# A convolutional gated MLP: the input scaled by 1/rms once, taps read from PSUM, and four of five down granules as seven block products

## What is computed

```
h = _rmsnorm(x, ffn_norm_g[l])
u = jnp.einsum('bsd,df->bsf', h, w_up[l])          # 1024 -> 2 * 2816
u = _causal_dwconv(u, conv_w[l], conv_b[l])        # y[t] = b + w0 u[t-2] + w1 u[t-1] + w2 u[t]
gate, val = jnp.split(u, 2, axis=-1)
x = x + jnp.einsum('bsf,fd->bsd', jax.nn.silu(gate) * val, w_down[l])
```

## Time and profile before

| | |
|---|---|
| median of 3 runs | 1955.98 us (1955.34 to 1956.61) |
| span of the profiled execution, first to last instruction | 1955.1 us |
| TensorE busy, share of the span | 1937.1 us, 99% |
| VectorE busy | 1419.4 us, 73% |
| ScalarE busy | 854.3 us, 44% |
| this MLP, with what lies just around it | 440 to 830 us of the span |

### The profile page before, as it was taken

The page is one execution under the profiler, slowest core; times in us unless marked ns, Lnnn a source line. Parts: engine busy times, 40 slices in busy tenths (PEclk is TensorE's granted clock), DMA queues, the critical chain, the costliest instruction groups (busy, mean ns, idle before and its releaser), DMA issues.

```text
span 1955.1 us, 24513 instructions
## 1 busy us (share of the span) xinstructions
PE 1937.1 (99%) x9769; PEld 1623.6 (83%) x9769; DVE 1419.4 (73%) x1983; ACT 854.3 (44%) x1343; POOL 123.8 (6%) x152
## 2 busy tenths in 40 slices
PE   9999999999999999999999999999999999999998
PEld 8887777888888888888888899998877888888886
DVE  6665687568656665846477788888898778887787
ACT  5453464335333334533222444444357655444443
POOL 1001240000000000000000010000024310000000
PEclk9999999999999999999999999999999999999999
DMA  5322212212323232332322432332223132332311
GB/s 177 108 87 65 89 63 87 86 43 88 108 91 104 87 107 87 108 108 87 108 72 80 137 106 87 112 116 76 76 62 105 44 118 68 127 108 87 108 65 65
DMA packets 139826, 181.14 MB, mean 93 GB/s; under 512 B 9792, under 2 KB 98496, under 8 KB 139712
## 3 DMA queue, kind: packets, MB, share of 16 engines
q1 hardware_dynamic: 137824, 178.04, 28.3%
q10 hardware_dynamic: 1632, 1.51, 0.2%
q0 software_dynamic: 256, 0.02, 0.0%
HBM read 177.44 MB, written 2.10 MB: 92 GB/s over the span
## 4 chain that ended last, share of the span: by engine, by line
PE 94%; DVE 3%; ACT 1%; issue 1%; POOL 0%; ACTq 0%; DVEq 0%; POOLq 0%
PE bank L751 21%; PE bank L753 21%; PE bank L752 20%; PE bank L1293 5%; PE bank L1291 5%; PE bank L1292 5%; PE bank L915 4%; PE bank L794 2%; PE bank L796 2%; PE bank L795 2%; PE bank L907 2%; PE bank L1005 1%; PE bank L993 1%; PE bank L1220 1%; DVE w_lo L1441 1%
## 5 line engine op out<-in xcount | busy, mean ns | idle before, releaser
L751 PE MATMUL bank<-h_hi,w_hi 128*128 128x512 f32 x1384 | 546.0, 395 | 2.1 <-DVE w_lo L1441 1.2
L753 PE MATMUL bank<-h_hi,w_lo 128*128 128x512 f32 x1384 | 539.2, 390 | 0.0
L752 PE MATMUL bank<-h_lo,w_hi 128*128 128x512 f32 x1384 | 538.8, 389 | 0.0
L2340 ACT ACTIVATE w_hi<-raw 128x1024 fp32r<-128x1024 f32 (+2 forms) x207 | 203.2, 1020 | 260.6 <-PE bank L753 207.3
L751 PEld LDWEIGHTS bank<-h_hi,w_hi 128*128 128x128 f32 x1384 | 259.9, 188 | 58.6 <-issue 3.0
L752 PEld LDWEIGHTS bank<-h_lo,w_hi 128*128 128x128 f32 x1384 | 260.0, 188 | 54.5 <-issue 2.1
L753 PEld LDWEIGHTS bank<-h_hi,w_lo 128*128 128x128 f32 x1384 | 259.8, 188 | 54.5
L1441 DVE TENSOR_TENSOR w_lo<-raw,w_hi 128x1024 fp32r<-128x1024 f32 (+2 forms) x195 | 235.9, 1241 | 34.0 <-ACT w_hi L2340 33.3
L751 PE MATMUL bank<-g_hi,w_hi 128*128 128x512 f32 (+1 forms) x460 | 177.9, 387 | 1.7 <-issue 1.0
L753 PE MATMUL bank<-g_hi,w_lo 128*128 128x512 f32 (+1 forms) x460 | 172.6, 375 | 0.0
L752 PE MATMUL bank<-g_lo,w_hi 128*128 128x512 f32 (+1 forms) x460 | 172.3, 375 | 0.0
(11 more groups left out here) (304 smaller groups left out, 3216.8 us busy)
## 6 DMA issues: line engine op xcount, KB each, us to landing
raw<-w SPq DMA_DIRECT2D x32, 1024.0 KB, 5.4
arena<-w SPq DMA_DIRECT2D x32, 1024.0 KB, 5.1
raw<-w_up SPq DMA_DIRECT2D x22, 1024.0 KB, 5.2
raw<-a_w_in SPq DMA_DIRECT2D x16, 1024.0 KB, 5.3
raw<-w_in SPq DMA_DIRECT2D x11, 1024.0 KB, 5.3
raw<-w_down SPq DMA_DIRECT2D x11, 1024.0 KB, 5.0
raw<-w_mkv SPq DMA_DIRECT2D x8, 1024.0 KB, 5.2
raw<-a_w_out SPq DMA_DIRECT2D x8, 1024.0 KB, 5.1
```

The source lines that it names most:

```text
L751: nc.tensor.matmul(dst, a_hi, b_hi, start=(k == 0), stop=False)
L752: nc.tensor.matmul(dst, a_hi, b_lo, start=False, stop=False)
L753: last = nc.tensor.matmul(dst, a_lo, b_hi, start=False, stop=(k == n - 1))
L2340: A(hi, src, ACT.Copy).then_inc(w_hi_done, 1)
```

## The change

- 1/rms is multiplied into `x * gain` once (8 tiles `h_scaled`), and `h_hi`, `h_lo` are made anew from it. The first pair still runs on the unscaled input, and its tiles are taken out with the multiplication. All later pairs run on the scaled input.
- The taps of these pairs are read from PSUM: ScalarE's last tap and VectorE's two others. VectorE's second one frees the bank (`tile_taken`).
- The down granules 0 to 3 are made of seven block products of 24 matmuls of 256 columns each, in the order P1, P2, P6, P4, P7, P5, P3. P3 and P4 are added to the residual at once, P5, P6 and P7 into sums in SBUF, P1 and P2 stay in banks; `gate_fold` adds them all at the end. Granule 4 and the 11th pair's chunk are made as before.

The diff, cut to its core. VectorE at the start, its taps, its place between the up tiles and the products of a granule (in `gate_granule`), the takes of the products, the fold, and what stands behind the granules:

```diff
+            def take_first_up():
+                def first_up(j):
                     take(lambda b: V.tensor_tensor(conv_u[:, j, 2:], b[:], rstd[:, 0, :], ALU.mult))
...
+                first_up(0)
+                scale_normed(range(0, 4))
+                first_up(1)
+                for j in range(2):
+                    gate_low("up", 0, j)
+                scale_normed(range(4, KT))
+                first_up(2)
+                for n in range(KT):
+                    low_half(h_lo[:, n, :], h_hi[:, n, :], h_scaled[:, n, :], None, h_ready)
+                first_up(3)
+                for j in range(2):
+                    gate_low("up", 1, j)
...
+            def up_tap(pair, j, between=lambda: None):
+                early = pair <= 2 * GATE_GRANULES
+                dve.wait_ge(act_out, acts.n + ((1, 2, 5, 6) if early else (1, 2, 3, 4))[j])
+                bank_of_up = tile_bank[tile.n % 4]
+                V.scalar_tensor_tensor(conv_y[:, j, 1:S], bank_of_up[:, 0:S - 1], w_col("conv_w1", pair, j),
+                                       conv_y[:, j, 1:S], ALU.mult, ALU.add).then_inc(tap_made, 1)
+                taps.n += 1
+                between()
+                dve.wait_ge(tap_made, taps.n)
+                take(lambda b: V.scalar_tensor_tensor(conv_y[:, j, 2:S], b[:, 0:S - 2], w_col("conv_w0", pair, j),
+                                                      conv_y[:, j, 2:S], ALU.mult, ALU.add))
...
+            def up_taps(pair):
+                for j in range(4):
+                    up_tap(pair, j, split_low if j % 2 else lambda: None)
...
+                up_tap(2 * n + 2, 2)
+                gate_low("P6", n)
+                up_tap(2 * n + 2, 3, lambda: gate_low("P4", n))
+                gate_low_left("P6", s2, lefts + 4)
...
+            def gate_take(n, name, t):
+                if name in ("P3", "P4"):
+                    dst = (by_half[1][0] if name == "P4" else by_half[0][1])[:, 2 * t:2 * t + 2, :]
+                    op = ALU.subtract if name == "P4" else ALU.add
+                    take(lambda bank: V.tensor_tensor(dst, dst, bank.rearrange("p (a b) -> p a b", b=256), op))
+                elif n == 0:
+                    take(lambda bank: V.tensor_copy(gate_sums[name][:, t, :], bank[:]))
+                else:
+                    take(lambda bank: V.tensor_tensor(gate_sums[name][:, t, :], bank[:], gate_sums[name][:, t, :], ALU.add))
...
+            def gate_fold():
+                p5, p6, p7 = [gate_sums[name].rearrange("p a (c n) -> p (a c) n", n=256) for name in ("P5", "P6", "P7")]
+                c11, c12, c21, c22 = by_half[0][0], by_half[0][1], by_half[1][0], by_half[1][1]
+                def in_order(dst, a, b):
+                    keep_order(V.tensor_tensor(dst, a, b, ALU.add))
+                dve.wait_ge(tile_taken, tile.n)
+                dve.wait_ge(gate_kept, 2 * GATE_GRANULES)
+                for dst in (c11, p6):
+                    for t in range(2):
+                        part = dst[:, 2 * t:2 * t + 2, :]
+                        in_order(part, KEPT["P1"][t].rearrange("p (a b) -> p a b", b=256), part)
+                settle()
+                for t in range(2):
+                    part = c11[:, 2 * t:2 * t + 2, :]
+                    V.tensor_tensor(part, KEPT["P2"][t].rearrange("p (a b) -> p a b", b=256), part, ALU.add)\
+                     .then_inc(gate_folded, 1)
+                in_order(c12, c12, p6)
+                in_order(p7, p7, p6)
+                settle()
+                in_order(c12, c12, p5)
+                in_order(c21, c21, p7)
+                in_order(c22, c22, p7)
+                settle()
+                keep_order(V.tensor_tensor(c22, c22, p5, ALU.add))
+                settle()
+                dve.wait_ge(gate_folded, 2)
...
+            gated_low(2 * GATE_GRANULES)
+            up_tap(9, 0)
+            gate_fold()
+            up_tap(9, 1, split_low)
+            up_tap(9, 2)
+            up_tap(9, 3, split_low)
+            gated(9)
+            gated_low(9)
+            up_taps(10)
+            gated(10)
             down(middle=lambda: gated_low(10))
             back("final, mix0")
```

ScalarE, high of a left operand, the place between the up tiles and the products of a granule, and pairs 9 and 10:

```diff
+            def gate_left_of(n, name, src, made_before, used):
+                if made_before:
+                    act.wait_ge(gate_left_made, 4 * n + made_before)
+                if used:
+                    act.wait_ge(*GATE_W.used_by[GATE_W.piece_at[used]])
+                A(left_form(g_hi, name), src, ACT.Copy).then_inc(gate_left_hi, 1)
...
+                up_tap(2 * n + 2, 2)
+                up_tap(2 * n + 2, 3)
+                gate_high("P6", n)
+                gate_high("P4", n)
+                gate_left_of(n, "P6", s2, 2, ("P1", n, 0))
...
+            def last_up(pair):
+                first = tile.n
                 for j in range(4):
                     if j % 2:
                         split_high()
...
+                    up_tap(pair, j)
```

TensorE:

```diff
+            def gate_product(n, name):
+                pe.wait_ge(w_split, GATE_W.lows(name, n))
+                pe.wait_ge(gate_left, 6 * n + GATE_LEFTS[name])
+                w_form = [GATE_W.ring(t, name, n).rearrange("p (k n) -> p k n", k=2) for t in (w_hi, w_lo)]
+                left = [left_form(t, name) for t in (g_hi, g_lo)]
+                kept = name in KEPT
+                if n == 0 and name == "P1":
+                    pe.wait_ge(std_done, stats.n)
+                for t in range(2):
+                    dst = (KEPT[name][t] if kept else next_bank())[:]
+                    for f in range(2):
+                        region = dst[:, 256 * f:256 * f + 256]
+                        cut = slice(P * (2 * t + f), P * (2 * t + f) + P)
+                        for k in range(2):
+                            (s_hi, s_lo), (m_hi, m_lo) = [x[:, k, cut] for x in w_form], [x[:, k, :] for x in left]
+                            begin = k == 0 and (n == 0 and f == 0 if kept else True)
+                            ends = k == 1 and (n == GATE_GRANULES - 1 or not kept)
+                            nc.tensor.matmul(region, s_hi, m_hi, start=begin, stop=False, skip_group_check=kept)
+                            nc.tensor.matmul(region, s_hi, m_lo, start=False, stop=False, skip_group_check=kept)
+                            last = nc.tensor.matmul(region, s_lo, m_hi, start=False, stop=ends, skip_group_check=kept)
+                    if not kept:
+                        full(last)
+                if kept:
+                    last.then_inc(gate_kept, 1)
...
+            for n in range(GATE_GRANULES):
+                for c in range(4 * n, 4 * n + 4):
+                    gate_up(c)
+                for name in PRODUCTS:
+                    gate_product(n, name)
+            for n in range(GATE_GRANULES, 5):
                 for c in range(4):
                     by_feature()
                 down()
```

More of the change, by code:

```diff
@@ L118, in weight_stream @@
     out += [g(0), v(0)]
-    for n in range(5):
+    before_gate = sum(item[0] not in ("tiles", "gate", "mlp1") for item in out)
+    out += [("gate", GATE_TILES)]
+    for n in range(GATE_GRANULES, 5):
         out += [g(2 * n + 1), v(2 * n + 1), g(2 * n + 2), v(2 * n + 2)] + down("w_down", n)
@@ L129, in weight_stream @@
         out += [first, ("tiles", 4 if n < 3 else 0), second]
-    not_shared = sum(item[0] not in ("tiles", "mlp1") for item in out)
+    not_shared = sum(item[0] not in ("tiles", "gate", "mlp1") for item in out)
     out += [("mlp1", MLP_TILES)]
@@ L135, in weight_stream @@
     out += [rows("b_w_o_2", c) for c in range(4)]
-    return out, not_shared
+    return out, not_shared, before_gate
 def build(nc, w, out):
@@ L772, in by_feature @@
                     parts = (range(0, 5), range(5, KT)) if j == 1 and between else (range(KT),)
+                    if passing and j == 1:
+                        parts = [range(k, k + 1) for k in range(KT)]
                     for part in parts:
@@ L775, in by_feature @@
                                          arrive if j == 0 else None, part)
-                        if part[-1] < KT - 1:
+                        if passing and j == 1:
+                            if part[-1] == KT - 1:
+                                tile.n += 1
+                                last.then_inc(tile_full, 1)
+                            else:
+                                last.then_inc(h_passed, 1)
+                        elif part[-1] < KT - 1:
                             between()
-                    full(last)
+                    if not (passing and j == 1):
+                        full(last)
                 if tiles == 2 or not pair:
@@ L2577, in _, with high_of_scaled, last_tap @@
             root(rstd[:, 0, :], None, stat_bank[:], None, D)
-            def up(granule):
+            def high_of_scaled():
+                for n in range(KT):
+                    act.wait_ge(tap_made, n + 1)
+                    if n < KT - 1:
+                        act.wait_ge(h_passed, n + 1)
```

(7 more changed lines are left out.)

326 lines of the change are left out of this document (278 added, 48 removed).

## The result

The changed kernel takes **1961.89 us** (median of 6 runs, 1961.29 to 1964.45); the kernel before, run beside it, 1956.2 us (6 runs, 1954.66 to 1956.66). The ratio is 1.0032, 95% interval 1.0022 to 1.0043: slower by 5.7 us. The forecast was 1962.5 us, slower.

What follows compares the result with a forecast made beforehand. TensorE, busy 99% of the span, was taken to bound the kernel. Waits of 12.0 us and 2.2 for the clock against 7.7 gained made 6.5 us more: 1962.5 us, range 1956.5 to 1965.5.

Steps and rivals of the forecast that it cites:

- Gross gain: TensorE's saving: 7.5 us from four granules of 63.70 instead of 65.58 us, 0.2 from a down gap; 7.7 us.
- The rival with half-paced products: Block products run at 0.1133 us a matmul, half the 512-column pace: 4.5 us less in all, 1958.0 us; chance 0.08.
- Wait 1: First scaled chunk: TensorE waits for the new `h_lo` of k = 0 behind VectorE's takes, scalings and lows; 1.6 us.
- Wait 2: Third up chunk, first granule: TensorE waits for the low completing the chunk, at the end of VectorE's unbroken chain; 1.7 us.
- Wait 3: P6 in each granule: its left low stands behind the last up tile's taps; 0.8 us, four times 3.2 us.
- wait 5: Granule 4's down: the fourth bank waits for VectorE's second tap, behind two highs and two lows; 4.9 us.
- Wait 4: The fold, from pair 9's start: VectorE's additions make the next chunk's lows late for TensorE; 0.6 us.
- The clock: TensorE's clock falls to half in granule 4's down wait, slowing work behind it; 2.2 us, bounds 0 and 2.95.
- The rival with an unchanged clock: The clock stays at full through the wait in granule 4's down: 1960.3 us; chance 0.18.
- The sum: Whole kernel: 12.0 us of waits and 2.2 for the clock against 7.7 gained: 6.5 us more, 1962.5 us.
- The taps from PSUM: Taps reading PSUM instead of SBUF cost VectorE no more; nothing added, against the skill's 0.065 us per tap.

Runs made afterwards that it cites:

- e9: Changed kernel with e4, e5, e7, pair 10's last-tile taps ahead of highs and lows, granule 4's first down chunk tile by tile, fold a tap later; 1948.95 us.
- e7: Changed kernel with VectorE's takes of the second and third unscaled tile moved behind the first `h_lo` and the last; 1962.84 us.
- e4: Changed kernel with VectorE's low of P6's weights between the last up tile's taps, P4's weight low behind P6's left low; 1958.94 us.
- e8: Changed kernel with two more VectorE additions of 1024 columns in each of four granules, results unread; 1962.89 us.
- e5: Changed kernel with the three sums of weight blocks moved behind the lows that complete the third up chunk; 1960.08 us.
- e3: Changed kernel with TensorE running 17 unread matmuls of 512 columns ahead of its wait for the fourth bank in granule 4's down; 1958.49 us.
- e2: Changed kernel with VectorE's taps of pair 10's last tile ahead of its two lows, ScalarE's order unchanged; 1959.17 us.

## Why the prediction was right, step by step

**Gross gain 7.7 us: right.** A granule is 64.36 us with a P6 wait of 0.66, so 63.70 without it, what the rows of the later MLP gave. The products take 537.51 − 516.70 − 0.66 = 20.15 us. The rival with half-paced products is out. e9, with few waits, brings the gain to light: 7.3 us by the medians, and in the trace 6.5 and the 1.2 of waits left.

**Wait 1, 1.6: measured 1.6. Wait 2, 1.7: measured 1.6.** Both are chains of VectorE instructions, fourteen and thirty-two of them, summed from four spacings; the sums held to 0.1 us. That they are one chain is seen in e7, where wait 2 grew by 0.7 as wait 1 shrank by 0.9 (from start to start), and the trace from the landmark on stayed at +6.1: the sum of the two is more certain than either.

**Wait 3, four times 0.8: measured four times 0.66.** The timelines of VectorE and ScalarE in the changed kernel, to lay beside the prediction's chain with T = 516.70 and, for wait 5, 774.51:

```profile
518.67 1.23 DVE L2035 TENSOR_TENSOR w_lo<-arena,w_hi 128x1024 fp32r<-128x1024 f32 x1 [4.26 <-ACT w_hi L2931]
519.81 0.74 DVE L2006 SCALAR_TENSOR_TENSOR arena<-bank,vec,arena 128x511 f32<-128x511 f32 x1
520.47 1.22 DVE L2035 TENSOR_TENSOR w_lo<-arena,w_hi 128x1024 fp32r<-128x1024 f32 x1
521.60 0.75 DVE L2011 SCALAR_TENSOR_TENSOR arena<-bank,vec,arena 128x510 f32<-128x510 f32 x1
522.26 0.69 DVE L2040 TENSOR_TENSOR g_lo<-arena,g_hi 128x512 fp32r<-128x512 f32 x1
...
777.47 0.75 DVE L2006 SCALAR_TENSOR_TENSOR arena<-bank,vec,arena 128x511 f32<-128x511 f32 x1 [5.76 <-ACT arena L2909]
778.14 2.35 DVE L1595 TENSOR_TENSOR w_lo<-raw,w_hi 128x1024 fp32r<-128x1024 f32 x2
780.41 0.74 DVE L2011 SCALAR_TENSOR_TENSOR arena<-bank,vec,arena 128x510 f32<-128x510 f32 x1
```

```profile
516.90 0.78 ACT L2909 ACTIVATE arena<-bank,vec 128x512 f32<-128x512 f32 x1 [4.06 <-PE bank L854]
517.58 2.00 ACT L2931 ACTIVATE w_hi<-arena 128x1024 fp32r<-128x1024 f32 x2
...
774.77 2.01 ACT L2659 ACTIVATE w_hi<-raw 128x1024 fp32r<-128x1024 f32 x2 [4.72 <-PE bank L854]
776.68 0.76 ACT L2909 ACTIVATE arena<-bank,vec 128x512 f32<-128x512 f32 x1
```

ScalarE began 0.20 behind the tile's end (0.25 was taken), its tap blocked it for 0.68 (0.72), and the rest came at the spacings of the sum. The low ended at 522.95, TensorE was at work at 523.05.

**Wait 4, 0.6: measured 0.3.** 752.59 − 752.13 − 0.23 = 0.23, and 0.1 for the matmul behind. The term was the small difference of two sums of 22 us, so being 0.3 off is no great error of the sums, and still half of the term.

**Wait 5, 4.9: measured 4.66.** Every link is in the rows: 0.26 to ScalarE, two highs 1.91, tap 0.79 to VectorE's start, tap 0.67, two lows 2.27, second tap 0.74, and 0.06 to TensorE (781.21), 6.70 in all where 6.9 was summed. The hand-over was priced at 0.22, with a late second matmul in it; that was most of the difference.

**The clock, 2.2: mis-sized, measured 2.97.** The mechanism was right, and the bound of 2.95 taken from the row at 233 us was the value in this execution. It had been cut because TensorE is fully busy on both sides of wait 5; that did not bring the clock back any sooner: 6.8 us at half here, 6.8 there. But there is no one price. Five profiles have this wait of 4.66 us: those of the change, e4, e7 and e8 have 5.6 to 6.1 us of work at half behind it, that of e5 has 3.4, so the term is 1.7 to 3.0 us. What decides between them no run here shows. The rival with an unchanged clock is out by the windows, and e3 shows what it would have been worth. The Trainium skill ("TensorE: Matmul & The Clock Gate", Part 1) has the clock fall when the engine is idle and activity bring it back; with both the trace agrees.

**The sum.** Waits 1.6 + 1.6 + 2.64 + 0.3 + 4.66 = 10.8, clock 2.97, gain 7.7: 6.1, as the trace has it, where 6.5 was forecast. Part of the closeness is chance: the waits were 1.2 us too long and the clock 0.8 too short.

**The taps from PSUM, nothing: right.** The means by form, first of the changed kernel, then of the kernel before:

```profile
L2011 DVE SCALAR_TENSOR_TENSOR arena<-bank,vec,arena 128x510 f32<-128x510 f32 x40 | 29.9, 746 | 0.7
...
L2909 ACT ACTIVATE arena<-bank,vec 128x512 f32<-128x512 f32 x40 | 30.7, 772 | 62.7 <-PE bank L854 62.7
```

```profile
L1823 DVE SCALAR_TENSOR_TENSOR arena<-arena,vec 128x512 f32<-128x512 f32 x44 | 30.1, 744 | 0.0
...
L2585 ACT ACTIVATE arena<-arena,vec 128x512 f32<-128x512 f32 x44 | 35.6, 808 | 48.5 <-DVE arena L1808 48.5
```

VectorE's taps take 746 ns from PSUM and 744 from SBUF. The Trainium skill ("VectorE: DVE Perf Modes", the section on the TRN2 errata) would have 0.065 us more for the first; no such thing is there. For ScalarE the same section has the PSUM source shorter, by 43 ns (52 cycles at 1.2 GHz); the trace has 36 (808 to 772).

## What to carry to other kernels

When work is taken off the engine that is the bound, write down for each hand-over which instruction of another engine frees its next bank or makes its next operand, and what stands ahead of that instruction: here the order at a few places took back all of a 7.7 us gain and 6 us more, on engines busy 75% and 45%, and 9 us of load added to one of them where it had room did nothing. A single idle stretch of TensorE can cost more than its length, if the clock falls and the work behind it runs at half rate: here 1.7 to 3.0 us more behind a wait of 4.66 us, 1.7 behind one of 2.5, nothing behind one of 2.3. So give such a term a range. A wait cured at the head of a full chain returns at its end, so the cures are to be timed together, not one by one.

## What the runs showed of the hardware that was not expected

- A wait of 2.5 us (e2, 776.69 to 779.20) between two fully busy stretches was enough for the clock to fall, right at its end; TensorE then ran at half for 3.3 us. Behind the 4.66 us wait it was 5.95 us in the changed kernel and 3.4 in e5, where the fall came 0.5 us after TensorE had begun again. The waits of up to 1.5 us in this MLP left it at full, and so did e7's of 2.3 us (494.05 to 496.54): 1.00 over 440 to 772 us.
- The clock fall at 232 to 240 us differs between executions of the same instructions, behind the same wait of 2.1 us: the clock there is 0.53 and 0.61 (before), 0.77 and 0.80 (the change), 1.00 and 1.00 (e3). It moved this MLP's start by 1.2 us between the two first profiles, nearly as much as one of the waits under study.
- VectorE took up eight more additions of 1024 columns, 9.1 us of its time, where it waits for up tiles, without a cost in the trace (e8).
